# In a mixed attention and recurrence kernel, two of the four copies that carry a turned tile across the partitions go from ScalarE to VectorE

## The chip, the cores and the metric

The kernel runs on one core of one Trainium2 chip. The time is device microseconds of one execution, as median of several: 3127.36 us before the change (3 runs, 3123.82 to 3134.74). One further execution was recorded by the hardware profiler; all rows below are of that one. A core has five engines that this text speaks of: TensorE (PE, its weight loads PEld), VectorE (DVE), ScalarE (ACT), GpSimd (POOL) and SyncE (SP, which issues most DMAs). Each runs its own list of instructions in order and waits at semaphores for the others.

## The reference

The program is a whole block of a network on a sequence of 1024 tokens, followed by a second one. Only one stage matters here, the RWKV-7 recurrence, run forward and backward over the sequence with 8 heads of 64 channels:

```python
def wkv7_scan(r, w, k, v, a, b, reverse):
    def step(state, inp):
        r_t, w_t, k_t, v_t, a_t, b_t = inp
        sa = jnp.einsum('bhvk,bhk->bhv', state, a_t)
        state = (state * w_t[:, :, None, :] + sa[..., None] * b_t[:, :, None, :]
                 + v_t[..., None] * k_t[:, :, None, :])
        return state, jnp.einsum('bhvk,bhk->bhv', state, r_t)
    _, out = lax.scan(step, s0, xs, reverse=reverse)
```

Beside it stands the latent attention of the same layer (8 heads, 8 blocks of 128 queries, softmax over 1024 keys). The two need nothing from each other. What follows (output projection, feed-forward network, second block) is dense matmuls.

## The kernel before

**The recurrence by chunks.** The sequence is cut into 8 tiles of 128 tokens, each two chunks of 64. Both directions ("ways", d = 0 and 1) go over the 8 tiles, way 1 in the other order. Inside a tile the recurrence becomes matrix algebra, and it needs the inverse of a triangular 64 x 64 matrix for each of the 16 pairs of chunk and head. The inverse is built by doubling: first blocks of 8 (steps `row0` to `spread`, on VectorE), then level 3, 4 and 5 (blocks of 16, 32, 64). A level lev has two steps. `Y`: TensorE multiplies (16 calls, 32 recorded matmuls, line 1422), VectorE masks the product (line 1656). `X`: TensorE multiplies again (line 1438, for level 5 line 1445), VectorE adds the product to the inverse (line 1663, for level 5 line 1667).

**The turn.** The inverse is wanted in both orientations, X and its transpose XT. Three times in a tile the present one is turned: after `spread` (step `X`, from XT to X), and with the steps `Y4` and `Y5` (from X to XT). `across_pe` (line 1350) makes four 128 x 128 transposes on TensorE into one PSUM bank. The result lies with heads and chunks crossed, so that it takes four copies of 64 partitions x 256 elements to bring it home, each from one half of the partitions to one half: `across_act` (line 1355), all four on ScalarE. The next matmul of that way waits for the fourth (`a.by(s, ..., 3)`), and so does whoever takes the PSUM bank next: the two ways share a ring of four banks (`wtake`).

There are 16 tiles (8 for each way), 3 turns in each, and so 48 turns and 192 copies.

**What sets the order.** Each engine's list is written by a planner (`slots`) that lays the steps of the two ways beside each other, way 1 thirteen steps behind way 0, and puts the parts of the attention between them (on TensorE `S` line 1795, `V` line 1806, `T` line 1818; on VectorE the maximum `M` line 1824 and the reciprocal `R` line 1827; on ScalarE the exponential line 1840, the scaling line 1844 and two copies lines 1835 and 1850). One round of 27 steps carries both ways over one tile; tables (`STEADY`, `HEAD`, `ENDING`) fix the order within a step for the steady part, the start and the end. A step's name calls the same step function on every engine, and an engine that has nothing to do in it writes nothing.

**Other steps in the text.** `scores` (TensorE line 1395, VectorE masks line 1611 x4), `PV` (TensorE line 1406, VectorE line 1618), `Nc` (lines 1626 to 1629), `mul` (lines 1598 to 1606), `S0` and `S1` (the state: TensorE 1506 and 1512, VectorE 1685, 1688 and, for half of the partitions, 1693), `post1` to `post3` (lines 1697 to 1723). At the end the next stage is mixed in: line 297 splits a weight panel, line 2136 makes `oalo`, line 2169 are its matmuls.

Of the kernel before, what the change touches and what calls it, by code (L numbers as in the profile page):

```python
# [213 lines left out]
def build(nc, A, out):  # L214
# [19 lines left out]
    def banks(aps):  # L234
        everything.append(Ring(aps))
        return everything[-1]
# [18 lines left out]
    def K(name, n, o=0):  # L255
        return cc[:, CC[name] + o:CC[name] + o + n]
# [981 lines left out]
    wring = banks(bank[0:4])  # L1238
# [48 lines left out]
    def cols(n):  # L1287
        return slice(64 * n, 64 * (n + 1))
# [7 lines left out]
    def part(ap, lev, s):  # L1296
        b_ = 1 << lev
        if len(ap.shape) == 2:
            return ap.rearrange("p (g s b) -> p g s b", s=2, b=b_)[:, :, s, :]
        return ap.rearrange("p h (g s b) -> p h g s b", s=2, b=b_)[:, :, :, s, :]  # L1300

    def packed(ap, lev):
        return ap[:, 0:256].rearrange("p (h g b) -> p h g b", h=8, b=1 << lev)
# [38 lines left out]
    def wtake(e, d, s, name, *empties):  # L1342
        ap, waits = wring.take((d, s, name), *empties)
        for w in waits:
            e.wait_ge(*w)
        return ap

    def across_pe(e, ap, M):
        for p in range(4):
            m = e.transpose(ap[:, 128 * p:128 * (p + 1)], M[:, :, :].rearrange("q h t -> q (h t)")[:, 128 * p:128 * (p + 1)], ident)  # L1350
        return m

    def across_act(e, M, ap, sig, *key):
        for n, (cc_, h) in enumerate(((0, 0), (1, 1), (0, 1), (1, 0))):
            e.activation(M[cols(cc_), :, :].rearrange("q (p h) t -> q p h t", h=2)[:, :, h, :],
                         ap.rearrange("q (p c t) -> q p c t", p=4, c=2)[cols(h), :, cc_, :], AF.Copy).then_inc(*sig.up(*key, n))

    def w_pe(e, d, s, c):
        x, t, v, a, g = D[d], t_w[d], v_w[d], a_w[d], g_w[d]
# [15 lines left out]
        if c == "turn":  # L1375
            for name, sig, empty in (("At", v, a), ("Rt", v, a), ("Bt", v, a), ("Kt", v, a)):
                ap = wtake(e, d, s, name, (empty, s, name + "T"))
# [6 lines left out]
        if c == "scores":  # L1384
            e.wait_ge(*a.by(s, "BtT"))
            for half in range(2):
                bb = [wtake(e, d, s, ("SC", half, h), (v, s, "SC", half, h)) for h in range(2)]
                for w, y in ((x.BT, 128), (x.KT, 0)):
                    if half == 0 and y == 0:
                        e.wait_ge(*a.by(s, "KtT"))  # L1390
                    for q in range(2):
                        p = 2 * half + q
# [5 lines left out]
        if c == "PV":  # L1398
            e.wait_ge(*v.by(s, "SC", 0, 1))
            ap = wtake(e, d, s, "PV", (a, s, "PV"))  # L1400
# [6 lines left out]
                                 start=True, stop=True)  # L1407
            m.then_inc(*t.up(s, "PV"))
        if c == "X":
            ap = wtake(e, d, s, "X", (a, s, "X", 3))  # L1410
            e.wait_ge(*v.by(s, "XT0"))
            across_pe(e, ap, x.XT).then_inc(*t.up(s, "X"))
        if c in ("Y3", "Y4", "Y5"):
            lev = int(c[1])
            if lev == 3:
                e.wait_ge(*a.by(s, "X", 3))
            else:
                e.wait_ge(*v.by(s, "X", lev - 1))
            ap = wtake(e, d, s, ("Y", lev), (v, s, "Y", lev))
            for i, (h, p) in enumerate(HH):  # L1420
                for cc_ in range(2):
                    m = e.matmul(ap[cols(cc_), 32 * i:32 * (i + 1)], x.SC[cols(cc_), p, BA, h, :],  # L1422
                                 part(x.X[cols(cc_), i, :], lev, d), start=True, stop=True)
            m.then_inc(*t.up(s, "Y", lev))
            if lev > 3:
                ap = wtake(e, d, s, ("XT", lev - 1), (a, s, "XT", lev - 1, 3))
                across_pe(e, ap, x.X).then_inc(*t.up(s, "XT", lev - 1))
        if c in ("X3", "X4", "X5"):
            lev = int(c[1])
            Y = x.Ys[lev]  # L1430
            e.wait_ge(*v.by(s, "Y", lev))
            if lev > 3:
                e.wait_ge(*a.by(s, "XT", lev - 1, 3))
            if lev < 5:
                ap = wtake(e, d, s, ("X", lev), (v, s, "X", lev))
                for i in range(8):
                    for cc_ in range(2):
                        m = e.matmul(ap[cols(cc_), 32 * i:32 * (i + 1)], x.XT[cols(cc_), i, :],  # L1438
                                     part(Y[cols(cc_), i, :], lev, d), start=True, stop=True)
                m.then_inc(*t.up(s, "X", lev))  # L1440
            else:
                ap = wtake(e, d, s, ("XT", lev), (v, s, "XT", lev))
                for i in range(8):
                    for cc_ in range(2):
                        m = e.matmul(ap[cols(cc_), 32 * i:32 * (i + 1)], Y[cols(cc_), i, :],
                                     part(x.XT[cols(cc_), i, :], lev, 1 - d), start=True, stop=True)
                m.then_inc(*t.up(s, "XT", lev))
# [44 lines left out]
        if c in ("S0", "S1"):  # L1492
            n = int(c[1])
            cc_ = n if d == 0 else 1 - n
            if n == 0:
                e.wait_ge(*v.by(s, "RG", 1))
            ap = wtake(e, d, s, ("S", n), (v, s, "S+", n))
# [18 lines left out]
    def w_act(e, d, s, c):  # L1516
# [38 lines left out]
        if c == "X":  # L1555
            e.wait_ge(*t.by(s, "X"))
            across_act(e, x.X, wring.bank(d, s, "X"), a, s, "X")
        if c in ("Y4", "Y5"):
            lev = int(c[1]) - 1
            e.wait_ge(*t.by(s, "XT", lev))  # L1560
            across_act(e, x.XT, wring.bank(d, s, ("XT", lev)), a, s, "XT", lev)
# [21 lines left out]
    def w_dve(e, d, s, c):  # L1583
        x, t, v, a, g = D[d], t_w[d], v_w[d], a_w[d], g_w[d]
# [57 lines left out]
        if c == "spread":  # L1642
            e.wait_ge(*v.by(s, "row", 7))
            if s:
                e.wait_ge(*t.by(s - 1, "WU", 1))
            e.tensor_tensor(x.XT[:, :, :].rearrange("p h (b t) -> p h b t", b=8),
                            x.Xc[:, :, None, :].broadcast_to([128, 8, 8, 8]),
                            K("bm", 64).rearrange("p (b t) -> p b t", b=8)[:, None, :, :].broadcast_to([128, 8, 8, 8]),
                            OP.mult).then_inc(*v.up(s, "XT0"))
        if c in ("Y3", "Y4", "Y5"):  # L1650
            lev = int(c[1])
            Y = x.Ys[lev]
            m = K("lmask", 32 >> lev, 7 * d + LMASK[lev])[:, None, :, None].broadcast_to([128, 8, 32 >> lev, 1 << lev])
            e.wait_ge(*t.by(s, "Y", lev))
            e.wait_ge(*g.by(s, "Y0", lev))
            e.tensor_tensor(part(Y, lev, d), packed(wring.bank(d, s, ("Y", lev)), lev), m,
                            OP.mult).then_inc(*v.up(s, "Y", lev))
        if c in ("X3", "X4", "X5"):
            lev = int(c[1])
            if lev < 5:  # L1660
                Xs = part(x.X[:, :, :], lev, d)
                e.wait_ge(*t.by(s, "X", lev))
                e.tensor_tensor(Xs, packed(wring.bank(d, s, ("X", lev)), lev), Xs, OP.add).then_inc(*v.up(s, "X", lev))
            else:
                Xs = part(x.XT[:, :, :], lev, 1 - d)
                e.wait_ge(*t.by(s, "XT", lev))
                e.tensor_tensor(Xs, packed(wring.bank(d, s, ("XT", lev)), lev), Xs, OP.add).then_inc(*v.up(s, "XT", lev))
# [10 lines left out]
        if c in ("S0", "S1"):  # L1678
            n = int(c[1])
            cc_ = n if d == 0 else 1 - n  # L1680
            q = cols(cc_)
# [195 lines left out]
    def way_calls():  # L1877
        made = [(0, "split")]
        for s in range(9):
            for c in BEFORE + BETWEEN + AFTER:  # L1880
# [105 lines left out]
    def scan_pe(e):  # L1986
        e.wait_ge(*v_pre.all())
        e.wait_ge(*a_pre.all())
        e.wait_ge(*v_gt.all())
        scan(e, "pe", w_pe, att_pe, tail_pe)  # L1990

    def scan_dve(e):
        pre_over(e)
        scan(e, "dve", w_dve, att_dve, tail_dve)
# [1506 lines left out]
```

## Time and profile before

| | us |
|---|---|
| median of 3 runs | 3127.36 |
| lowest and highest run | 3123.82, 3134.74 |
| the profiled execution | 3123.17 |
| its span (first to last instruction) | 3121.4 |
| TensorE busy | 3047.4 (98%) |
| VectorE busy | 2038.7 (65%) |
| ScalarE busy | 1126.4 (36%) |
| GpSimd busy | 410.6 (13%) |
| mean granted TensorE clock | 0.994 |

The recurrence with the attention beside it takes from about 540 to 1225 us of the span; the turns lie between 568 and 1202 us. A row of a timeline gives the start in us from the start of the span, the length in us, the engine, the line, the operation with its tiles (out<-in), the shape, and how many equal instructions it merges; behind it, in brackets, the idle time of the engine ahead of it, and who ended it. "issue" means that the engine waited for nothing that the profile shows. The length of a matmul is modelled, so between matmuls the starts are compared.

### The profile page before, as it was taken

How to read it: one execution, taken by the hardware profiler on the slowest of the kernel's cores; microseconds unless marked ns; L12 is line 12 of the kernel's file. 1: busy time of each engine (PE TensorE's matmuls, PEld its weight loads, DVE VectorE, ACT ScalarE, POOL GpSimd, SP SyncE). 2: the span in 40 equal slices, each digit the busy share in tenths (PEclk: the TensorE clock that was granted, in tenths of full speed). 3: DMA queues.
4: the chain of work that ended last, by engine and by line, in shares of the span. 5: the costliest groups of instructions: out<-in, count | busy, mean ns of one | idle time of the engine just before them, and what ended most of it. 6: DMA issues, size and time to landing. Idle time of an engine off the chain costs nothing.

```text
span 3121.4 us, 52257 instructions
## 1 busy us (share of the span) xinstructions
PE 3047.4 (98%) x21972; PEld 2482.2 (80%) x21972; DVE 2038.7 (65%) x3118; ACT 1126.4 (36%) x1667; POOL 410.6 (13%) x467
## 2 busy tenths in 40 slices
PE   7999999899999999999999999999999999999999
PEld 7887887677777777888888888888776888788887
DVE  5666554477777675546556555698789999664454
ACT  5222334566666553223222222200144333433332
POOL 0232442011110001402221221100000000100000
PEclk9999999999999999999999999999999999999999
DMA  4333666223232223425545553566511223223222
GB/s 153 122 136 102 218 225 208 66 76 91 75 94 77 80 93 114 155 81 211 194 189 202 198 195 146 229 248 252 201 68 68 94 95 108 90 88 121 107 94 81
DMA packets 121754, 424.98 MB, mean 136 GB/s; under 512 B 15536, under 2 KB 41776, under 8 KB 94128
## 3 DMA queue, kind: packets, MB, share of 16 engines
q1 hardware_dynamic: 86880, 295.26, 26.9%
q0 software_dynamic: 34640, 126.37, 11.0%
q8 instruction: 175, 2.87, 0.4%
q14 instruction: 59, 0.48, 0.1%
HBM read 311.48 MB, written 110.10 MB: 135 GB/s over the span
## 4 chain that ended last, share of the span: by engine, by line
PE 82%; DVE 10%; ACT 3%; issue 2%; POOL 1%; DMA 1%; SPq 0%; DVEq 0%; ACTq 0%; POOLq 0%
PE ps L2645 29%; PE ps L321 15%; PE ps L505 8%; PE ps L2453 4%; PE ps L1795 3%; PE ps L2355 3%; PE ps L1818 2%; DVE Yh L2846 2%; PE ps L1422 2%; PE ps L1806 2%; PE ps L2169 1%; PE ps L1028 1%; PE ps L1438 1%; PE ps L1382 1%; DVE wlo L297 1%
## 5 line engine op out<-in xcount | busy, mean ns | idle before, releaser
L293 ACT ACTIVATE whi<-raw 128x2048 fp32r<-128x2048 f32 x131 | 250.4, 1911 | 385.9 <-PE ps L2645 189.8
L297 DVE TENSOR_TENSOR wlo<-raw,whi 128x2048 fp32r<-128x2048 f32 x131 | 300.7, 2295 | 87.3 <-ACT whi L293 86.9
L2846 DVE SCALAR_TENSOR_TENSOR Yh<-uT,vc,Yh 128x512 f32<-128x512 f32 x472 | 335.6, 747 | 4.0
L2645 PE MATMUL ps<-Hh,whi 128*128 128x512 f32 x1024 | 317.1, 391 | 0.6 <-DVE wlo L297 0.6
L2645 PEld LDWEIGHTS ps<-Hh,whi 128*128 128x128 f32 x1024 | 192.1, 188 | 42.7 <-issue 1.9
L321 PE MATMUL ps<-Hhi,whi 128*128 128x512 f32 x672 | 206.9, 389 | 0.0
L321 PE MATMUL ps<-Hlo,whi 128*128 128x512 f32 x672 | 206.9, 389 | 0.0
L321 PE MATMUL ps<-Hhi,wlo 128*128 128x512 f32 x672 | 206.8, 389 | 0.0
L2645 PE MATMUL ps<-aHh,whi 128*128 128x512 f32 x512 | 199.7, 390 | 0.1
L2645 PE MATMUL ps<-Hh,wlo 128*128 128x512 f32 x512 | 199.2, 389 | 0.0
L2645 PE MATMUL ps<-aHh,wlo 128*128 128x512 f32 x512 | 199.2, 389 | 0.0
L2645 PE MATMUL ps<-aLh,whi 128*128 128x512 f32 x512 | 199.2, 389 | 0.0
L2645 PE MATMUL ps<-Gh,whi 128*128 128x512 f32 x576 | 180.3, 394 | 2.9 <-DVE wlo L297 2.9
L3030 DVE TENSOR_TENSOR xT<-ps,xT 128x512 f32<-128x512 f32 x256 | 168.8, 685 | 19.1 <-PE ps L2645 19.1
L505 PE MATMUL ps<-Hhi,whi 128*128 128x512 f32 (+1 forms) x512 | 163.1, 400 | 0.0
L505 PE MATMUL ps<-Hlo,whi 128*128 128x512 f32 (+1 forms) x512 | 158.6, 391 | 0.0
L505 PE MATMUL ps<-Hhi,wlo 128*128 128x512 f32 (+1 forms) x512 | 157.9, 390 | 0.0
L321 PEld LDWEIGHTS ps<-Hlo,whi 128*128 128x128 f32 x672 | 126.1, 188 | 26.2
L321 PEld LDWEIGHTS ps<-Hhi,whi 128*128 128x128 f32 x672 | 126.1, 188 | 26.2
L321 PEld LDWEIGHTS ps<-Hhi,wlo 128*128 128x128 f32 x672 | 126.1, 188 | 26.2
L3014 DVE TENSOR_TENSOR aLh<-rth,aHh 128x512 fp32r<-128x512 f32 x64 | 41.3, 687 | 143.9 <-ACT aHh L3008 143.8
L1795 PE MATMUL ps<-Kp,Qb 96*128 96x512 f32 x256 | 128.8, 626 | 5.6 <-ACT Pb L1840 4.2
(417 smaller groups left out, 6394.4 us busy)
## 6 DMA issues: line engine op xcount, KB each, us to landing
raw<-in_panels SPq DMA_DIRECT2D x131, 1024.0 KB, 4.8
whi<-sph SPq DMA_DIRECT2D x28, 1024.0 KB, 4.8
wlo<-spl SPq DMA_DIRECT2D x28, 1024.0 KB, 6.9
rwf<-F POOLq DMA_DIRECT2D x16, 1280.0 KB, 6.5
sraw<-in_panels POOLq DMA_DIRECT2D x40, 512.0 KB, 4.4
sph<-shi POOLq DMA_DIRECT2D x40, 512.0 KB, 4.5
spl<-slo POOLq DMA_DIRECT2D x40, 512.0 KB, 5.2
L<-rwf SPq DMA_DIRECT2D x16, 1024.0 KB, 6.4
```

What stands on the lines that cost most here:

```text
L293: e.activation(whi[i % 2][:, :], raw_of(i)[:, :], AF.Copy).then_inc(*a_hi.up(i))
L297: e.tensor_tensor(wlo[i % 2][:, :], raw_of(i)[:, :], whi[i % 2][:, :].bitcast(F32), OP.subtract).then_inc(*v_lo.up(i))
L321: m = e.matmul(aps[h][0:n1 - n0, :], w[wi][:, kc, n0:n1], mov[mi][:, kc, hs(h)], start=x == 0 and q == 0, stop=x == len(kcs) - 1 and q == 2)
L505: m = e.matmul(aps[h][0:n1 - n0, :], W[wi][:, kc, n0:n1], H2[mi][:, kc, hs(h)], start=kc == 0 and q == 0, stop=kc == 7 and q == 2)
L1422: m = e.matmul(ap[cols(cc_), 32 * i:32 * (i + 1)], x.SC[cols(cc_), p, BA, h, :], part(x.X[cols(cc_), i, :], lev, d), start=True, stop=True)
L1795: m = e.matmul(bank[4 + half], Qb[g % 3][:, h, :], Kp[k % 2][:, h, hs(half)], start=True, stop=True)
L1806: m = e.matmul(bank[7][64 * n:64 * n + 64, 128 * (w % 4):128 * (w % 4) + 128], Vp[(w // 8) % 2][:, i, 64 * n:64 * n + 64], PT[:, i, n, :], ...
L2355: m = e.matmul(aps[h], W[wi][:, kc, n0:n0 + 128], H2[mi][:, kc, hs(h)], start=kc == 0 and q == 0, stop=kc == 7 and q == 2)
L2453: m = e.matmul(ap, W[wi][:, kc, 128 * n:128 * n + 128], (aH, aL)[mi][b % 2][:, kc, :], start=kc == 0 and q == 0, stop=kc == 1 and q == 2)
L2645: m = e.matmul(ap, W[wi][:, kc, n0:n0 + 128], mov[mi][:, kc, :], start=x == 0 and q == 0, stop=x == len(kcs) - 1 and q == 2)
L2846: e.scalar_tensor_tensor(out=to, in0=x, scalar=w, in1=to, op0=OP.mult, op1=OP.add).then_inc(*v_e.up(*key))
L3030: e.tensor_tensor(xT[:, n, hs(h)], ring.bank("x", h, b, n), xT[:, n, hs(h)], OP.add).then_inc(*v_e.up("x", h, b, n))
```

## The change

The four copies are parted by the half of the partitions that they read. ScalarE keeps the two that read partitions 0 to 63, VectorE gets the two that read 64 to 127 (one of them writes the upper half, one the lower). Who waited for ScalarE's fourth copy now waits for ScalarE's second and VectorE's second. On VectorE the copies stand in step `X` (which it had not taken part in), and in `Y4` and `Y5` right behind the mask. The planner is not changed, except that VectorE's table of the end names step `X` of way 1's last tile.

```diff
     def across_act(e, M, ap, sig, *key):
-        for n, (cc_, h) in enumerate(((0, 0), (1, 1), (0, 1), (1, 0))):
+        for n, (cc_, h) in enumerate(((0, 0), (1, 0))):
             e.activation(M[cols(cc_), :, :].rearrange("q (p h) t -> q p h t", h=2)[:, :, h, :],
                          ap.rearrange("q (p c t) -> q p c t", p=4, c=2)[cols(h), :, cc_, :], AF.Copy).then_inc(*sig.up(*key, n))
+
+    def across_dve(e, M, ap, sig, *key):
+        for n, (cc_, h) in enumerate(((1, 1), (0, 1))):
+            e.tensor_copy(M[cols(cc_), :, :].rearrange("q (p h) t -> q p h t", h=2)[:, :, h, :],
+                          ap.rearrange("q (p c t) -> q p c t", p=4, c=2)[cols(h), :, cc_, :]).then_inc(*sig.up(*key, n))
...
         if c == "X":
-            ap = wtake(e, d, s, "X", (a, s, "X", 3))
+            ap = wtake(e, d, s, "X", (a, s, "X", 1), (v, s, "X0", 1))
...
             if lev == 3:
-                e.wait_ge(*a.by(s, "X", 3))
+                e.wait_ge(*a.by(s, "X", 1))
+                e.wait_ge(*v.by(s, "X0", 1))
...
             if lev > 3:
-                ap = wtake(e, d, s, ("XT", lev - 1), (a, s, "XT", lev - 1, 3))
+                ap = wtake(e, d, s, ("XT", lev - 1), (a, s, "XT", lev - 1, 1), (v, s, "XTc", lev - 1, 1))
...
             if lev > 3:
-                e.wait_ge(*a.by(s, "XT", lev - 1, 3))
+                e.wait_ge(*a.by(s, "XT", lev - 1, 1))
+                e.wait_ge(*v.by(s, "XTc", lev - 1, 1))
...
+        if c == "X":
+            e.wait_ge(*t.by(s, "X"))
+            across_dve(e, x.X, wring.bank(d, s, "X"), v, s, "X0")
...
+            if lev > 3:
+                e.wait_ge(*t.by(s, "XT", lev - 1))
+                across_dve(e, x.XT, wring.bank(d, s, ("XT", lev - 1)), v, s, "XTc", lev - 1)
...
-                -20: ((1, 7, "spread"), (0, 7, "RG"), (1, 6, "post2")), -19: (), -18: ((0, 7, "S0"), (1, 7, "Y3")),
+                -20: ((1, 7, "spread"), (0, 7, "RG"), (1, 6, "post2")), -19: ((1, 7, "X"),), -18: ((0, 7, "S0"), (1, 7, "Y3")),
```

Where this puts the copies is seen best at two places of VectorE's list. The first is in the steady part, once in every round: the `scores` masks of way 1 (tile SC1), then the attention's maximum (st_m), `PV` of way 1 (E11), the level 3 mask of way 0 (Y30), `Nc` of way 1, and the level 3 addition of way 0 (X0). The number at the end of a name is the buffer's, a 0 or 1 ahead of it the way. Before:

```order
L1611 TENSOR_TENSOR SC1_156<-ps,cc_49 128x2x4x64 x4
L1824 TENSOR_REDUCE st_m_178<-ps 128x1
L1618 TENSOR_TENSOR E11_152<-SC1_156,cc_49 128x512
L1656 TENSOR_TENSOR Y30_124<-ps,cc_49 128x32x8
L1626 TENSOR_REDUCE Nc1_168<-E11_152 128x64
L1628 TENSOR_TENSOR Nc1_168<-Nc1_168,cc_49 128x64
L1629 COPY Xc1_169<-cc_49 128x64
L1663 TENSOR_TENSOR X0_122<-ps,X0_122 128x32x8
```

And in the changed kernel, whose line numbers are 7 to 13 higher:

```order
L1618 TENSOR_TENSOR SC1_156<-ps,cc_49 128x2x4x64 x4
L1360 COPY X0_122<-ps 64x4x64 x2
L1837 TENSOR_REDUCE st_m_178<-ps 128x1
L1625 TENSOR_TENSOR E11_152<-SC1_156,cc_49 128x512
L1666 TENSOR_TENSOR Y30_124<-ps,cc_49 128x32x8
L1633 TENSOR_REDUCE Nc1_168<-E11_152 128x64
L1635 TENSOR_TENSOR Nc1_168<-Nc1_168,cc_49 128x64
L1636 COPY Xc1_169<-cc_49 128x64
L1676 TENSOR_TENSOR X0_122<-ps,X0_122 128x32x8
```

The two copies of way 0's X stand behind the four masks and ahead of the maximum and of way 0's own mask. The second place is the end of the recurrence, on VectorE too: `post2` (sc1), the split of the next stage's weight panel (wlo0), the state of way 0 (St01), its output (Os0) and way 1's level 3 mask (Y31). Before:

```order
L1706 TENSOR_SCALAR sc1_167<-sc1_167 128x8
L297 TENSOR_TENSOR wlo0_56<-raw0_51,whi0_54 128x2048
L1685 TENSOR_TENSOR St01_139<-ps,H0_136 128x256
L1688 TENSOR_TENSOR St01_139<-St01_139,sc0_140 128x256
L1693 TENSOR_TENSOR Os0_137<-ps,Os0_137 64x4x64 x2
```

And in the changed kernel:

```order
L1719 TENSOR_SCALAR sc1_167<-sc1_167 128x8
L1360 COPY X1_149<-ps 64x4x64 x2
L297 TENSOR_TENSOR wlo0_56<-raw0_51,whi0_54 128x2048
L1698 TENSOR_TENSOR St01_139<-ps,H0_136 128x256
L1701 TENSOR_TENSOR St01_139<-St01_139,sc0_140 128x256
```

The copies, which wait for TensorE's transposes, now stand ahead of the panel's split, which waited for ScalarE alone.

## Rows read from the trace of the kernel before

**Rows 1.** Windows: length, busy (x) of PE, PEld, DVE, ACT, POOL; clock, DMA share, GB/s.
```profile
800.00:880.00 80.00, 78.87 (x1420) 63.10 (x1418) 56.44 (x124) 50.94 (x97) 8.00 (x11) 1.00 0.29 88
...
1060.00:1080.00 20.00, 16.40 (x302) 13.35 (x304) 11.72 (x27) 9.57 (x21) 0.21 (x1) 0.83 0.38 118
```
**Rows 2.** Line 1355, copies into XT: duration ns min/median/max, first and last start, forms.
```profile
L1355 ACT ACTIVATE XT<-ps x128: 375/378/381, 582.2 to 1200.5; 64x256 f32<-64x256 f32 x128
```
**Rows 3.** VectorE's copy of line 1671, same columns.
```profile
L1671 DVE COPY WU<-ps x16: 691/692/692, 603.7 to 1206.6; 128x512 f32<-128x512 f32 x16
```
**Rows 4.** Timeline of VectorE, 819 to 833 us, and one row at 982 us.
```profile
819.56 2.48 DVE L1611 TENSOR_TENSOR SC<-ps,cc 128x512 f32<-128x512 f32 x4 [0.58 <-PE ps L1395]
...
823.09 0.68 DVE L1618 TENSOR_TENSOR E<-SC,cc 128x512 f32<-128x512 f32 x1
823.81 0.42 DVE L1656 TENSOR_TENSOR Y<-ps,cc 128x256 f32<-128x256 f32 x1
...
826.41 0.42 DVE L1688 TENSOR_TENSOR St<-St,sc 128x256 f32<-128x256 f32 x1
826.87 0.77 DVE L1693 TENSOR_TENSOR Os<-ps,Os 64x256 f32<-64x256 f32 x2
827.67 0.42 DVE L1656 TENSOR_TENSOR Y<-ps,cc 128x256 f32<-128x256 f32 x1
...
831.70 0.42 DVE L1688 TENSOR_TENSOR St<-St,sc 128x256 f32<-128x256 f32 x1
832.04 0.74 DVE L1693 TENSOR_TENSOR Os<-ps,Os 64x256 f32<-64x256 f32 x2
832.71 0.41 DVE L1656 TENSOR_TENSOR E<-ps,cc 128x256 f32<-128x256 f32 x1
...
981.86 0.42 DVE L1656 TENSOR_TENSOR Y<-ps,cc 128x256 f32<-128x256 f32 x1 [0.36 <-PE ps L1422]
```
**Rows 5.** Timeline of TensorE: one round earlier, and beside the first rows of group 4.
```profile
743.89 1.12 PE L1422 MATMUL ps<-X,SC 64*64 64x32 f32 x32
...
822.64 1.12 PE L1422 MATMUL ps<-X,SC 64*64 64x32 f32 x32
...
824.29 1.12 PE L1438 MATMUL ps<-Y,XT 64*64 64x32 f32 x32
```
**Rows 6.** Timeline, VectorE and TensorE, around way 1's step X.
```profile
855.08 0.69 DVE L1606 TENSOR_TENSOR Kt<-L,E 128x512 f32<-128x512 f32 x1
...
856.49 1.12 PE L1422 MATMUL ps<-X,SC 64*64 64x32 f32 x32
```
**Rows 7.** Timeline, ScalarE and TensorE, around way 1's last turn of a tile.
```profile
873.77 1.58 ACT L1355 ACTIVATE XT<-ps 64x256 f32<-64x256 f32 x4 [1.80 <-PE ps L1350]
...
874.74 0.66 PE L1818 MATMUL ps<-cc,Pb 128*128 128x128 f32 x4
875.50 1.12 PE L1445 MATMUL ps<-XT,E 64*64 64x32 f32 x32
```
**Rows 8.** Timeline of TensorE in the first tile of way 0.
```profile
572.20 1.12 PE L1422 MATMUL ps<-X,SC 64*64 64x32 f32 x32 [0.75 <-ACT X L1355]
...
593.91 0.67 PE L1395 MATMUL ps<-AR,BT 64*64 64x128 f32 x16 [0.73 <-ACT XT L1355]
```
**Rows 9.** Timeline of TensorE, two gaps that nothing in the profile ends.
```profile
985.81 0.54 PE L1422 MATMUL ps<-X,SC 64*64 64x32 f32 x13 [0.89 <-issue]
...
1068.82 1.91 PE L1422 MATMUL ps<-X,SC 64*64 64x32 f32 x30 [3.26 <-issue]
```
**Rows 10.** Timeline at the end of the recurrence, TensorE and VectorE.
```profile
1159.94 1.12 PE L1445 MATMUL ps<-XT,E 64*64 64x32 f32 x32 [0.69 <-ACT XT L1355]
...
1169.89 2.32 DVE L297 TENSOR_TENSOR wlo<-raw,whi 128x2048 fp32r<-128x2048 f32 x1
1170.23 0.65 PE L1350 MATMUL ps<-cc,XT 128*128 128x128 f32 x4
...
1187.38 0.73 PE L2169 MATMUL ps<-oalo,whi 128*128 128x512 f32 x2 [0.40 <-DVE oalo L2136]
```

## The prediction

> **What bounds the kernel.** First the windows: in a steady stretch of 80 us TensorE is busy for 78.87, VectorE for 56.44, ScalarE for 50.94 [rows 1]. TensorE has some 1.1 us in 80 to give back, so halving a copy's latency can bring little. Harm has more room: whatever makes TensorE wait lengthens the span one for one. Next the copies themselves: ScalarE takes 378 ns for one [rows 2] and 1.58 us for four [rows 7]. Then the timelines of TensorE and VectorE around each of the six turns of one round (both ways, one tile each; 743.89 to 822.64, 78.75 us [rows 5]), to see what ends last ahead of the next matmul. The stretch that matters is VectorE's from 819.56 to 828.09: from the masks of `scores` on it is never idle (the bracket at 819.56 is the last until 829.62) [rows 4], and TensorE's level 3 matmuls start right on its heels: the mask of line 1656 ends at 823.81 + 0.42 = 824.23 and line 1438 starts at 824.29 [rows 4, 5]. Here VectorE is the bound, though it is busy for only 71% of the 80 us.
>
> **What the change removes.** 96 copies leave ScalarE, 96 x 0.378 = 36 us of its time, and a turn's latency there falls from 1.58 to about 0.78. ScalarE ends few waits of TensorE, so this pays only at the places named below.
>
> **What a copy costs VectorE.** The trace has no such copy there. Bounds: the addition of line 1693 has the same size, reads PSUM, and takes 0.77 or 0.74 for two, 0.41 each with the overlap [rows 4]; the copy of twice the elements takes 0.69 [rows 3]. The new copy reads one input, so I take 0.42, near line 1693; the range is 0.35 to 0.69.
>
> How close do they follow each other? Two rows of the same pair of instructions answer: in way 1's `S0` line 1688 starts at 826.41 and line 1693 at 826.87, 0.46 later; in `S1` it is 831.70 and 832.04, 0.34 later. The instruction behind starts 0.80 after line 1693 in the first case (827.67) and 0.67 in the second (832.71) [rows 4]. By the code (`q = cols(cc_)`) the first works on partitions 64 to 127, the second on 0 to 63, and all around them start at partition 0. So a change of the half costs 0.12 to 0.13 going in and as much coming out. Both new copies read the upper half, one writes the upper and one the lower, and their neighbours start at partition 0: each copy starts only when what precedes it has ended, and so does the next instruction that reads PSUM. I take 0.46 from copy to copy and to the next PSUM reader, and 0.12 ahead of the first where it has not waited anyway: 2 x 0.46 + 0.12 = 1.04 us of VectorE's list for a pair ahead of a PSUM reader, instead of 2 x 0.34 = 0.68.
>
> The Trainium skill (VectorE: DVE Perf Modes, Two Vector instructions with no wait between them) says the same as a rule: an instruction is held until all earlier ones have finished if its input or output begins in another quadrant of 32 partitions than the last one's did. The trace agrees, by the 0.46 against 0.34. With the rule the sum is the one below, +4.6 us; without it, +1.2.
>
> **Steady rounds, turn by turn.**
>
> Way 0's step X (tiles 1 to 4). The masks of line 1611 end at 819.56 + 2.48 = 822.04. In the new list the pair stands behind them: 822.08 to 822.95. TensorE's line 1422 started at 822.64 [rows 5] and now starts at 823.01, +0.37. But the maximum, line 1618 and the level 3 mask, back to back in front of line 1438, move by 1.04; the mask had waited 0.12 (823.81 against 823.09 + 0.60), so it comes 0.92 later, and line 1438 with it. The rest of VectorE's run follows at the same distance, so nothing is caught up: 4 x 0.92 = +3.7. The attention's maximum is 1.04 late as well, and ScalarE's exponential with it; TensorE's next `S`, which waits for the exponential, stands behind levels 3 and 4 and doesn't notice.
>
> The same step in tiles 5 and 6. There the mask waits 0.36 for TensorE (981.86) [rows 4], the delay would be 0.6 (1.04 less the 0.36 and its start-up), and soon after TensorE stands still for 0.89 and 3.26 us with nothing to release it [rows 9]. I read these as waits for its own instructions: another 0.6 us of lateness disappears in them. I take 0, with both ends at the third rival. In tile 7 no maximum follows, and I take 0.
>
> Way 1's step X. The pair stands behind line 1606, which ends at 855.77: 855.81 to 856.68. Line 1422 started at 856.49 [rows 6] and now at 856.74: +0.25, seven times: +1.75. The pair delays besides only `R`, which isn't urgent: ScalarE has four copies of `turn` to do before it scales.
>
> Way 1's step Y5. TensorE's line 1445 started at 875.50, when ScalarE's four copies were done at 873.77 + 1.58 = 875.35; the transposes of line 1818 end by their modelled length at 874.74 + 0.66 = 875.40, and what is behind them can start 0.1 before that modelled end or right at it [rows 7]. VectorE's pair ends at about 874.65, in time. Between 0.10 and 0.20 are won, I take 0.15: 7 x -0.15 = -1.05.
>
> The other three turns of a round have a long group of attention matmuls (`S` or `V`) behind them, and the pair ends before it does: 0.
>
> **Start.** In tile 0 of way 0 VectorE is idle, and TensorE waits 0.75 and 0.73 for line 1355 [rows 8]. Both waits nearly go: -0.6 and -0.7, -1.3.
>
> **End.** At 1159.94 TensorE waited 0.69 for the copies [rows 10], and gets 0.38 of it back, since the pair, in VectorE's list ahead of way 1's `S1`, makes the level 5 addition about 0.3 later (my estimate from 2 x 0.46). Then line 297, which started at 1169.89, must wait behind the copies for TensorE's transposes at 1170.23 + 0.65, 0.38 earlier by then: 1170.50, copies to 1171.4, so line 297 starts 1.57 late. The state and output behind it absorb most, but 0.3 reaches level 3, and the next pair (level 3 into XT) with its 1.1 us stands ahead of `post3` and line 2136, for which TensorE waits until 1187.38 [rows 10]: together +1.4 to +1.5 there, against the level before this stretch. I take +1.45; with the second pair hidden it would be +0.3.
>
> **The sum.** 3.7 + 0 + 1.75 - 1.05 - 1.3 + 1.45 = +4.55 us. TensorE also gets 48 more wait instructions; the profile shows no price for one ahead of a matmul that is queued in time, and I take 0, at most 0.02 each, 1 us. The profiled execution took 3123.17 (the span and 1.8 around it), which makes 3127.7. The median shown is 4.2 above it, since the runs lie between 3123.82 and 3134.74; from it the sum gives 3131.9. I say 3130, between the two.
>
> **Rivals.**
>
> *VectorE takes them in its stride.* If copies follow at 0.34 as `S1`'s neighbours do, the steady places cost 4 x (0.68 - 0.12) = 2.2 and 7 x 0.1 = 0.7, the end 0.6, the gains stay at -2.35: +1.15, or, with tiles 1 to 4 covered by something unseen, -1: 3122 to 3126. For it: 23 us of idle VectorE in 80. Against it: the two distances in rows 4. 17%.
>
> *Slower: VectorE's list is the bound, not only at one turn.* A pair (1.04, or 1.6 with the 0.69 copy) reaches TensorE at way 0's step X in all six tiles and at way 1's step X in full: 6 x 0.92 + 7 x 1.04 + 1.45 - 1.3 - 1.05 = +11.9 us, 3135 to 3141. It decides where `turn`'s and `scores`' ScalarE copies are not ready before the delayed matmul, or where a copy takes over 0.5 us. For it: the run without idle time. Against: around 856 only line 1422 stands behind the pair. 18%.
>
> *The two unexplained gaps move.* The one at 1068.82 is dear: the granted clock of its 20 us is 0.83 [rows 1], so for (1 - 0.83) x 20 / 0.5 = 6.8 us of them TensorE was at 1.2 instead of 2.4 GHz, after it had idled for 3.26. That is at most 3.26 + 3.4 = 6.7 us, of which I take 6. The added waits move TensorE's instruction stream by some places against its loads. If this gap goes, the sum is -1.5, 3121 to 3126; if another such one comes, +10.5, 3134 to 3138. For it: both gaps fall into the same matmul group of neighbouring rounds [rows 9], so place matters. Against: the stream moves by under 50 instructions. 13%.
>
> **Chances.** 52% for the forecast with its own range of 3125 to 3136, 17, 18 and 13 for the rivals. The range of 8 in 10 is 3120 to 3141. A difference under 0.3% (9.4 us) can't be told from none in this kernel. Slower by more than that is most of the second rival, part of the third and a tail of the forecast, 0.20; faster needs the first rival and a vanished gap together, 0.07; within it 0.73.
>
> **What will show it.** A pair of copies that takes 0.87 to 0.9 us from start to end and is followed at 0.46 by the maximum; VectorE's level 3 mask of way 0 starting about 5.2 us after the first of the four score masks did, instead of 4.25; an idle time of TensorE ahead of line 1438's successor of about 0.5 us, ended by VectorE, in tiles 1 to 4, and none in other steady turns; a round of 79.8 instead of 78.75 us; line 1445 0.15 us closer to the transposes before it; ScalarE's busy time 36 us less, VectorE's 40 more. The forecast is wrong if a copy takes over 0.6 us, if the round stays at 78.75, or if the 3.26 us gap isn't there.

## The result and the profile after

The changed kernel took 3137.86 us (median of 18 runs, 3125.72 to 3152.9), the kernel before 3129.26 (18 runs, 3116.76 to 3138.18): ratio 1.0034, 95% interval [1.0021, 1.0047]. By the ratio that is 10.6 us slower (interval 6.6 to 14.7; the two medians lie 8.6 apart), where the forecast's sum was +4.55. The time lies in the range of 3120 to 3141, but outside the forecast's own 3125 to 3136. What came is the second rival, VectorE's list being the bound at more than one turn (+11.9, 3135 to 3141), to which 18% was given.

The profiled execution of the changed kernel took 3133.26 us, its span 3131.5. ScalarE is busy for 1091.0 us and VectorE for 2078.8. In the window of [rows 1] TensorE lost 1.47 us of busy time and VectorE gained 4.99:

```profile
800.00:880.00 80.00, 77.40 (x1392) 61.55 (x1389) 61.43 (x136) 45.04 (x84) 8.00 (x11) 1.00 0.27 83
```

The new copies, in the columns of [rows 2]. A VectorE copy takes 427 ns, 0.42 was taken:

```profile
L1360 DVE COPY XT<-ps x64: 425/427/428, 581.2 to 1210.2; 64x256 f32<-64x256 f32 x64
L1360 DVE COPY X<-ps x32: 425/427/428, 568.9 to 1178.7; 64x256 f32<-64x256 f32 x32
```

Way 0's step X, the stretch of [rows 4] (lines of VectorE's steps have moved, 1656 to 1666, 1611 to 1618, 1824 to 1837; TensorE's 1422 to 1428 and 1438 to 1445). Timeline of VectorE, changed kernel (start and length in us, engine, line, operation, and in brackets the idle time before it and what ended it):

```profile
819.24 2.48 DVE L1618 TENSOR_TENSOR SC<-ps,cc 128x512 f32<-128x512 f32 x4 [0.58 <-PE ps L1400]
821.75 0.88 DVE L1360 COPY X<-ps 64x256 f32<-64x256 f32 x2
822.67 1.23 DVE L1837 TENSOR_REDUCE st_m<-ps 128x1 f32<-128x1024 f32 x1
823.81 0.68 DVE L1625 TENSOR_TENSOR E<-SC,cc 128x512 f32<-128x512 f32 x1
824.41 0.42 DVE L1666 TENSOR_TENSOR Y<-ps,cc 128x256 f32<-128x256 f32 x1
```

and TensorE beside it:

```profile
822.74 1.12 PE L1428 MATMUL ps<-X,SC 64*64 64x32 f32 x32 [0.28 <-issue]
823.79 0.66 PE L1831 MATMUL ps<-cc,Pb 128*128 128x128 f32 x4
824.88 1.12 PE L1445 MATMUL ps<-Y,XT 64*64 64x32 f32 x32 [0.43 <-DVE Y L1666]
```

The pair takes 0.88, the maximum starts 0.92 after the pair did (two pitches of 0.46), and the level 3 mask starts 824.41 - 819.24 = 5.17 us after the first score mask (5.2 forecast, 4.25 before). TensorE has two idle times there that it did not have, 0.28 and 0.43. The profile names nobody for the first, but VectorE's pair ends at 821.75 + 0.88 = 822.63 and line 1428, which waits for it, starts at 822.74. Counted from the first score mask, the matmuls behind the level 3 mask start after 824.88 - 819.24 = 5.64 us, before the change after 824.29 - 819.56 = 4.73: +0.91.

Way 1's step X, the stretch of [rows 6], TensorE and VectorE:

```profile
854.82 0.66 PE L1387 MATMUL ps<-cc,AP 128*128 128x128 f32 x4 [0.20 <-ACT E L1539]
855.31 0.60 PE L1387 MATMUL ps<-cc,Rt 128*128 128x128 f32 x4
855.87 0.63 PE L1387 MATMUL ps<-cc,SC 128*128 128x128 f32 x4
857.34 0.63 PE L1387 MATMUL ps<-cc,Kt 128*128 128x128 f32 x4 [0.84 <-DVE X L1360]
```
```profile
855.64 0.68 DVE L1613 TENSOR_TENSOR Kt<-L,E 128x512 f32<-128x512 f32 x1
856.35 0.88 DVE L1360 COPY X<-ps 64x256 f32<-64x256 f32 x2
```

This wait was not forecast. TensorE's transposes of Kt start when VectorE's second copy has ended (856.35 + 0.88 = 857.23). The reason is in the code: both ways take their PSUM banks from one ring of four, in the order in which TensorE's program asks. Way 1's X takes a bank, way 0's At, Rt and Bt (AP, Rt and SC in the rows) the other three, and Kt comes round to the one that X is still being copied from. The waits of TensorE over the whole span (us in total, times, longest) show it seven times, and a second new wait six times:

```profile
PE ps L1387 <- DVE X L1360: 5.9, 7, 0.8
...
PE ps L1445 <- DVE Y L1666: 2.6, 6, 0.4
```

The steady round is measured here from one tile of way 1 to its next, between the starts of the "spread transposes" (line 1350 reading XT, which is step X behind `spread`). Timeline of TensorE, before, then changed:

```profile
695.95 0.63 PE L1350 MATMUL ps<-cc,XT 128*128 128x128 f32 x4 [0.28 <-DVE XT L1646]
774.68 0.63 PE L1350 MATMUL ps<-cc,XT 128*128 128x128 f32 x4 [0.20 <-DVE XT L1646]
853.43 0.63 PE L1350 MATMUL ps<-cc,XT 128*128 128x128 f32 x4 [0.20 <-DVE XT L1646]
```
```profile
693.37 0.63 PE L1350 MATMUL ps<-cc,XT 128*128 128x128 f32 x4 [0.27 <-DVE XT L1653]
773.72 0.63 PE L1350 MATMUL ps<-cc,XT 128*128 128x128 f32 x4 [0.21 <-DVE XT L1653]
853.99 0.63 PE L1350 MATMUL ps<-cc,XT 128*128 128x128 f32 x4 [0.21 <-DVE XT L1653]
```

78.73 and 78.75 before, 80.35 and 80.27 changed: +1.6 a round, where +1.05 was forecast.

The gaps of [rows 9] (idle times of TensorE that the profile puts to "issue") are not the same ones. The 3.26 us one is gone (there is one of 0.49 at 1078.18, ahead of another line), and near the 0.89 one stands:

```profile
989.30 1.71 PE L1428 MATMUL ps<-X,SC 64*64 64x32 f32 x28 [1.08 <-issue]
```

with half the clock behind it, which before's 990 to 1000 did not have (windows, columns as in [rows 1]):

```profile
990.00:1000.00 10.00, 10.00 (x115) 7.40 (x115) 4.49 (x9) 1.96 (x4) 0.00 (x0) 0.50 0.27 66
```

### The profile page after: what moved, and what is told of

Read it like the earlier page. It is cut to its first block, busy times and chain, and to the rows that moved or that the text cites. A ratio compares the mean times of both kernels' runs of the same rounds, so it can differ in the third digit from the quotient of the medians.

```text
span 3131.5 us, 52305 instructions
## 1 busy us (share of the span) xinstructions
PE 3051.8 (97%) x21972; PEld 2487.2 (79%) x21972; DVE 2078.8 (66%) x3214; ACT 1091.0 (35%) x1571; POOL 410.6 (13%) x467
## 4 chain that ended last, share of the span: by engine, by line
PE 79%; DVE 13%; issue 3%; ACT 3%; POOL 1%; DMA 1%; SPq 0%; DVEq 0%; ACTq 0%; POOLq 0%
PE ps L2658 29%; PE ps L321 15%; PE ps L505 7%; PE ps L2466 4%; PE ps L1808 3%; PE ps L2368 3%; DVE Yh L2859 2%; PE ps L1819 1%; PE ps L1428 1%; PE ps L2182 1%; PE ps L1831 1%; PE ps L1028 1%; PE ps L1445 1%; DVE wlo L297 1%; DVE st_m L1837 1%
```

## The experiments

What has to be told apart is what a profile alone leaves mixed: the price of each pair, and gaps and clock. "Round" is the steady round as above. In the expectations A is the theory that step X's two places hold the loss and XT's pairs are free, B that every pair on VectorE costs alike. Each of the kernels is compared in times with the kernel before on its own chip.

**Step X on ScalarE alone, XT split.** In all variants of this kind a function says for which ways and steps the copies are parted, and waits follow it:

```diff
+    def parted(d, s, step):
+        return False if step == "X" else True
-            across_act(e, x.X, wring.bank(d, s, "X"), a, s, "X")
+            across_act(e, x.X, wring.bank(d, s, "X"), a, s, "X", both=parted(d, s, "X"))
-        if c == "X":
+        if c == "X" and parted(d, s, "X"):
             e.wait_ge(*t.by(s, "X"))
```

> The XT copies stay split, step X is back on ScalarE alone (four copies there) in both ways. The measure is the steady round, the distance between the spread transposes of successive tiles (L1350): 78.75 us in the kernel before, 80.3 us changed. Theory A (PSUM bank and list): of the +1.6 us a round about 0.8 us is the wait of PE's Kt transposes for the two VectorE copies of way 1's step X (0.84 us at 857.34), about 0.75 us is VectorE's list behind way 0's pair, and the XT pairs cost nothing: round 78.6 to 78.9 us here. Rival B (VectorE's load as such: six pairs a round, each at a like price of 0.27 us): round 79.8 us. Rival C (the round is not what matters, only the two issue gaps around 985 and 1075): total as in the changed kernel. In total under A: 5 to 8 us under the changed kernel if the gap at 989 goes, else 4 to 5 us over that; and as tile 0's gain at the start (4 us under C's and A's count alike) hangs on tile 0's step X, the total would be within 3 us of the kernel before.

Ratio 0.9994 [0.9978, 1.0011], 12 runs. Rounds of 78.61 and 78.58 in the profile, and 79.25 in the one that has an issue gap (0.28 at 697.08), which explains less than half of the difference. A holds, B (79.8) falls: 32 pairs on VectorE cost nothing in the round. The two short rounds are 0.15 under before's 78.74, the size of the forecast's term for way 1's Y5, but the time as a whole is not told apart from before's.

```profile
612.22 0.63 PE L1350 MATMUL ps<-cc,XT 128*128 128x128 f32 x4 [0.88 <-DVE XT L1662]
690.83 0.63 PE L1350 MATMUL ps<-cc,XT 128*128 128x128 f32 x4 [0.28 <-DVE XT L1662]
```

**Step X split in way 0 only** (`return d == 0 if step == "X" else True`).

> Step X is split in way 0 only, way 1's four copies are on ScalarE as before, XT split in both. Theory A: no PE wait for VectorE's X copies at the Kt transposes (changed kernel: 5.9 us in 7 waits), way 0's price of about 0.75 us stays: round 79.4 to 79.6 us against 80.3. Rival B (each pair alike at 0.27): round 80.0 us, and the wait at the Kt transposes may go without the round getting shorter, because VectorE's list would be the next to be late. Start gain of tile 0 (4 us by the first spread transpose, 613.11 against 617.15) kept if it is way 0's, gone if it is way 1's.

Ratio 1.0024 [1.0009, 1.004]. Rounds 79.54, 80.00, 79.50: the two short ones are 0.92 above the last kernel's short ones (78.60), which is the price forecast for this turn. For the 80.00 its profile shows no further wait; rounds of one profile differ by up to some 0.5 us in this way, so a price read from them is good to a few tenths. The wait at the Kt transposes is gone (its row has no bracket), so A's reading of that place holds:

```profile
859.54 0.63 PE L1390 MATMUL ps<-cc,Kt 128*128 128x128 f32 x4
```

**Step X split in way 1 only** (`d == 1`).

> Step X is split in way 1 only, XT split in both. Theory A: the wait at the Kt transposes stays (about 0.8 us, 7 times), the waits behind way 0's pair (PE L1445 for VectorE's SC, 0.4 us in 6 places) go: round 79.5 to 79.7 us. Rival B: 80.0 us.

Ratio 1.0021 [1.0005, 1.0037]. Rounds 79.50, 79.30, 79.59: 0.85 above 78.6, as A has it. The waits behind way 0's pair are gone, that at Kt stays (from 690 to 1010 us):

```profile
PE ps L1390 <- DVE X L1363: 3.4, 4, 0.8
```

**The halves exchanged.**

```diff
-        for n, (cc_, h) in enumerate(((1, 1), (0, 1))):
+        for n, (cc_, h) in enumerate(((0, 0), (1, 0))):
             e.tensor_copy(...)
```

ScalarE takes the other two, (1, 1) and (0, 1).

> The same split as in the changed kernel, but the engines change halves: VectorE copies what lies in the lower PSUM partitions, ScalarE the upper. If the hold between instructions that change the half of the partitions (pitch 0.46 against 0.34 us) is what delays the list behind way 0's pair, that saves one such change there, 0.12 us: masks at 5.05 us behind the first score mask (5.17 changed), round 80.1 to 80.2 us. If the hold is of no weight here: 80.3 us, the same total.

Ratio 1.0034 [1.0017, 1.0051]. Rounds from 80.15 to 80.88: in the time the small term isn't told apart. In the places it is there. Timeline of VectorE:

```profile
824.47 2.48 DVE L1627 TENSOR_TENSOR SC<-ps,cc 128x512 f32<-128x512 f32 x4 [0.58 <-PE ps L1403]
826.86 0.86 DVE L1363 COPY X<-ps 64x256 f32<-64x256 f32 x2
827.75 1.23 DVE L1846 TENSOR_REDUCE st_m<-ps 128x1 f32<-128x1024 f32 x1
829.49 0.42 DVE L1675 TENSOR_TENSOR Y<-ps,cc 128x256 f32<-128x256 f32 x1
```

The mask starts 829.49 - 824.47 = 5.02 us after the first score mask (5.05 expected, 5.17 in the changed kernel), and the wait at the Kt transposes is 0.70 instead of 0.84; one hold less would give both. Part of it goes into another wait of the round (line 1840 for ScalarE's PT, 0.66; 0.52 in the changed kernel).

**One instruction earlier in way 1.**

```diff
+            if d == 0 and s:
+                w_dve(e, 1, s - 1, "early")      # way 1's two copies
             e.tensor_tensor(x.Kt[:, :], k_, x.E2[:, :], OP.mult).then_inc(*v.up(s, "Kt"))
...
-        if c == "X":
+        if c == ("early" if d and s < 7 else "X"):
```

> The changed kernel; in way 1 VectorE makes step X's two copies one instruction earlier, ahead of way 0's Kt product instead of behind it. If the PSUM bank alone were what TensorE's Kt transposes wait for, the copies' earlier end (0.6 us) would shorten the wait from 0.84 to about 0.2 us and the round from 80.3 to 79.7 us. If it is VectorE's list (the transposes want the bank and the product, and VectorE makes both), the wait is then for the Kt product and stays 0.7 to 0.8 us, the round 80.2 us.

Ratio 1.0025 [1.0004, 1.0046], rounds 80.31 and 80.32. The bank is free earlier, and the same transposes now wait as long for the product, which VectorE makes behind the copies. Timeline of TensorE and of VectorE:

```profile
866.46 0.63 PE L1387 MATMUL ps<-cc,Kt 128*128 128x128 f32 x4 [0.89 <-DVE Kt L1615]
```
```profile
864.84 0.89 DVE L1360 COPY X<-ps 64x256 f32<-64x256 f32 x2
865.64 0.68 DVE L1615 TENSOR_TENSOR Kt<-L,E 128x512 f32<-128x512 f32 x1
```

So the bank is only where it shows. VectorE has to make four products and two copies before these transposes, and which of the last two comes first doesn't matter; on ScalarE the copies lay beside the products.

**Step X split in both ways, XT on ScalarE alone** (`return step == "X"`).

> Step X is split in both ways, XT is on ScalarE alone. If prices add (way 0's step X 0.83 us a round by e_x0 less e_xt, way 1's 0.53 by e_x1 less e_xt, XT 0.18 by e_xt less the kernel before): round 78.74 + 0.83 + 0.53 = 80.1 us, ratio 1.003. Rival (VectorE's load at large): a third of the pairs of a round, 78.74 + 1.57/3 = 79.3 us, ratio 1.001.

Ratio 1.0025 [1.0008, 1.0041]. Rounds of 80.49 and 80.46 without a gap over 0.3 us, others longer by gaps of up to 2.3; 80.1 was expected from the sum, 79.3 by load. Load falls; the sum is near, a little low. With the prices as read from the short rounds, 0.92 and 0.85, it is 78.74 + 0.92 + 0.85 = 80.5.

**The issue gaps.** Waits were put at the very start of TensorE's program, where it stands idle for 13.7 us, to move its instruction stream. That idle time was too short for them. In the ten profiles without them TensorE's first matmul starts between 12.56 and 13.86 us, with 322 of them at 20.87, with 250 at 17.13 and 16.90; so 72 waits more take some 3.8 us, 0.05 each. The delay is still there at 520 us: the attention's first `S` starts at 528.5, 524.0 and 523.4 us, against 519.2 to 521.3 in the others. The ratios of the three padded kernels therefore hold 7 and 4 us (0.23% and 0.13%) that have nothing to do with gaps.

```diff
     def mla_pe(e):
+        for _ in range(322):
+            e.wait_ge(*d_vec.by())
```

> The kernel before, with 322 further waits (161 instructions) at the start of TensorE's program, on a load that has landed long before its first matmul at 13.7 us; nothing else is changed. Theory F: the issue gaps (0.89 us at 985.81, 3.26 us at 1068.82) come where TensorE's instruction stream reaches a certain count (I count 256 instructions between such places) while a large load is under way, so a program moved by 161 instructions has none there, and keeps the clock behind them: 7 us less than before (ratio 0.9977), the profile without a gap over 0.5 us from 960 to 1100. Rival: the gaps belong to the place in the work or are chance: the same gaps or others like them, ratio 0.999 to 1.001.

Ratio 1.0012 [0.9993, 1.0031]; less the 7 us of late start it would be some 0.999 ±0.002, and there neither theory F's 0.9977 nor the rival's 0.999 to 1.001 is excluded. From 960 to 1100 us there is indeed no gap, but there are eight from 635 to 952 instead, 0.34 to 0.97 long, such as

```profile
678.40 0.88 PE L1424 MATMUL ps<-X,SC 64*64 64x32 f32 x23 [0.97 <-issue]
```

Moving the stream moved the gaps. What they take in all in this one profile, 5.0 us between 540 and 1225, is not less than before's 4.1. Whether the expected 7 us were there, this kernel can't show.

The same in the changed kernel (250 waits):

> The changed kernel with 250 further waits (125 instructions) at the start of TensorE's program. Theory F: no gap at 989 (1.08 us) and 1078 (0.49 us), full clock from 990 to 1010, 5 to 7 us less than the changed kernel (ratio to before 1.0012 to 1.0018), while the round stays 80.3 us: the round, not the gaps, holds what the change costs. Rival (the change's loss lies in the gaps, which only its extra instructions moved): ratio to the kernel before 1.000. Rival (gaps are chance): 1.0034 as the changed kernel.

Ratio 1.003 [1.0009, 1.0051], less the 4 us of late start some 1.0018. That is the upper end of theory F's range, but with ±0.002 the rival's 1.0034 isn't excluded. Rounds 80.20 and 80.28: no gap is left from 960 to 1100 and the round is as long as ever, so what the round costs isn't in those gaps. But now the clock fell at another place, without any long gap ahead of it (windows):

```profile
820.00:830.00 10.00, 9.22 (x200) 7.55 (x200) 8.85 (x19) 5.62 (x10) 2.07 (x4) 0.93 0.64 225
830.00:840.00 10.00, 10.00 (x116) 7.39 (x112) 4.82 (x10) 3.10 (x6) 0.00 (x0) 0.50 0.15 38
```

And with step X on ScalarE:

> Step X on ScalarE alone, XT copies split, and 250 further waits at the start of TensorE's program. Theory F with theory A: round 78.7 to 78.9 us, no gap over 0.5 us between 960 and 1100: ratio to the kernel before 0.997 to 0.9985, the fastest of all. Rival (gaps are chance): 0.9994 as without the waits.

Ratio 1.0005 [0.9984, 1.0025], rounds 79.16, 79.04 and 78.97, and a gap of 2.24 at 948.77. Less the late start this is some 0.999, which again lies between theory F's 0.997 to 0.9985 and the rival's 0.9994. That no gap over 0.5 us stands from 960 to 1100 came true; a gain isn't shown.

**Two repeats.** First all copies on ScalarE again (`return False`), then the changed kernel.

> All copies on ScalarE, as in the kernel before: the same instructions in the same order. If the two issue gaps of the kernel before (0.89 us at 985.81, 3.26 us at 1068.82) come from the program's layout, they come again at these places within 0.5 us of their length; if they are chance in place or length, this profile has others, and the steady round is 78.7 us either way.

Ratio 0.999 [0.9978, 1.0003]. A round of 78.82, and gaps in the same instruction stream of which the first is not before's:

```profile
705.62 3.78 PE L1817 MATMUL ps<-Kp,Qb 96*128 96x512 f32 x4 [3.02 <-issue]
...
996.40 0.54 PE L1434 MATMUL ps<-X,SC 64*64 64x32 f32 x13 [1.99 <-issue]
...
1077.22 1.11 PE L1434 MATMUL ps<-X,SC 64*64 64x32 f32 x30 [0.80 <-issue]
```

The last two stand ahead of the same pieces, x13 and x30, as in [rows 9], but are 1.99 and 0.80 long where they were 0.89 and 3.26. Three more, of 0.87, 1.04 and 0.36 us, stand at 626.34, 916.48 and 1034.05, where before had none. So a gap can come again at its place with another length, and others come and go. The length varies from run to run; the program may set where a gap can be, but not that there is one.

> The changed kernel once more, for its profile. Round 80.3 us again, wait at the Kt transposes 0.84 us again. The first spread transpose at 613.1 us if tile 0's gain is the change's, up to 618 us if it hung on the clock there; a gap near 989 us and half the clock behind it again if they are the program's, elsewhere if not.

3145.79 us in one run. The 1.08 us gap near 989 is not there. Rounds 80.21 and 80.27, Kt waits 0.8 each; way 1's first spread transpose at 615.73. From 630 to 1080 us no issue gap is over 0.28, and yet the clock is at half twice, behind the same turn of two tiles (windows):

```profile
670.00:680.00 10.00, 10.00 (x113) 7.39 (x112) 4.82 (x10) 2.70 (x6) 0.00 (x0) 0.50 0.15 38
...
920.00:930.00 10.00, 10.00 (x112) 7.39 (x112) 4.85 (x11) 1.96 (x4) 0.00 (x0) 0.50 0.15 38
```

**The clock apart from the rest.** Every run has its time and its mean granted clock. Their product is roughly what the run would take at full clock, and the rest what the clock took; the clock is recorded to 0.001, or 3 us a run, so only means say something. Means over the runs, with the standard error of the mean:

| kernel | runs | time x clock | lost to the clock |
|---|---|---|---|
| before (three chips) | 93 | 3105.0 to 3105.6, each ±0.6 or less | 21.7 to 23.1 ±1.1 |
| all on ScalarE again | 10 | 3105.1 ±0.7 | 20.6 ±1.4 |
| XT split alone | 12 | 3104.9 ±0.5 | 19.8 ±1.6 |
| way 0's X and XT | 12 | 3107.6 ±0.7 | 26.7 ±1.9 |
| way 1's X and XT | 12 | 3110.3 ±0.5 | 21.9 ±1.5 |
| X alone, both ways | 12 | 3114.6 ±0.6 | 21.4 ±2.3 |
| changed | 19 | 3112.6 ±0.6 | 26.3 ±1.6 |
| halves exchanged | 12 | 3112.1 ±0.7 | 24.8 ±1.5 |
| one instruction earlier | 12 | 3111.7 ±0.2 | 23.3 ±1.4 |
| before, 322 waits | 12 | 3112.1 ±0.5 | 18.0 ±1.5 |
| changed, 250 waits | 12 | 3112.9 ±0.7 | 22.8 ±2.4 |
| XT split alone, 250 waits | 12 | 3106.5 ±0.7 | 20.9 ±2.0 |

Against XT alone, way 1's step X costs 5.4 us of full-clock time and 2.1 ±2.2 of clock, way 0's 2.7 and 6.9 ±2.5. Together 8.1 of full-clock time, and the changed kernel has 7.7: the prices add. Against before the changed kernel has 7.3 us more of full-clock time, which stands well outside the errors (the two variants of it that ran on one chip with the kernel before, halves exchanged and one instruction earlier, have 6.5 and 6.7), and 4.0 ±1.7 more of clock. The clock's share is the weaker one. The five other kernels with way 0's step X split lose between 21.4 and 26.7 us to it. All 79 runs with that step split, the changed kernel's among them, lose 24.4 ±0.8, all 151 without 21.5 ±0.5: 2.9 ±0.9, and not 6.9, is what way 0's step X takes through the clock over all kernels. The 7 us of full-clock time of "before, 322 waits" are its late start.

## Why the prediction came out as it did

- **Copy, pitch, list of way 0: right.** 0.427 for 0.42, 0.46 for 0.46, the mask at 5.17 for 5.2, the matmuls behind it 0.91 later for 0.92, and 0.92 a round by the experiment. That an instruction is held when its input or output begins in another quadrant of 32 partitions than the last one's, as the Trainium skill (VectorE: DVE Perf Modes, Two Vector instructions with no wait between them) says, agrees with the 0.46 here and with the exchange of halves, which has one such change less and put the mask at 5.02. That this hold matters for the time the exchange couldn't show.
- **Way 0, tiles 5 and 6 taken as 0: wrong.** The new wait of 0.43 is there six times, at 986.05 and 1076.08 too. That the gaps would hide the lateness was argued from [rows 9]; 2 x 0.92 = 1.8 us were missed by it, if a round there pays what a steady one does.
- **Way 1's step X, 7 x 0.25: the step that failed.** The forecast put only line 1422 behind the pair, and wrote against its rival that "around 856 only line 1422 stands behind the pair". Between Kt's product and line 1422 stand the Kt transposes, and they need the bank that the pair reads. Measured: 5.9 us in seven waits, 0.85 a round by experiment, so 7 x 0.85 = 5.95 for 1.75, which is 4.2 us missed. Two rows of the kernel before that the forecast did not use, TensorE's and ScalarE's, had it:

```profile
855.92 0.63 PE L1382 MATMUL ps<-cc,Kt 128*128 128x128 f32 x4
```
```profile
854.13 1.59 ACT L1355 ACTIVATE X<-ps 64x256 f32<-64x256 f32 x4
```

  ScalarE's four copies had freed the bank at 855.72, 0.2 ahead of the transposes. The new pair can't start before VectorE's products are done at 855.77 [rows 6].
- **Way 1's Y5, -0.15 each: right in size.** The matmuls of line 1452 now start 0.58 us after the transposes ahead of them (876.67, 876.09), 0.76 before: -0.18. The round with XT alone split is 0.15 shorter than before's.
- **Start, -1.3: about right.** Both waits of [rows 8] are gone. The 4 us by which way 1's first spread transpose came earlier in the profile (613.11 for 617.15) are not the change's: between 580 and 590 us the clock was 0.86 instead of 0.51. With the clock at a like level there (0.52 and 0.54) the repeats of both kernels have 615.73 and 616.79, -1.1; counted from way 0's first spread transposes, at 568.37 and 567.54, it is -1.9.
- **End, +1.45: not contradicted.** From line 1350 of the last tile (1099.47, 1106.61) to the span's end it is 2021.9 before and 2024.9 changed, +3.0, of which 1.5 are the clock's at 1180 to 1190 (0.85). The wait of 0.69 at 1159.94 is gone, a new one of 0.79 stands at 1181.81, ended by `St`, and the four at line 2182 have 0.63 as the longest. The same stretch takes 2021.5 and 2023.4 in the other two profiles with all copies on ScalarE, and from 2022.9 to 2027.3 in the others with pairs on VectorE, so no run tells 1.45 from 0.3 or from 3.
- **The gaps as a rival: half right.** Their places move with the stream, but the two runs of one stream gave other lengths and partly other places, so a case built on one profile's gap vanishing or not was no property of the change.
- **The signs.** The forecast named three that would show it wrong, and one of them came: the 3.26 us gap isn't there. After the repeats this says nothing on the copies. The signs that did speak were two others: a wait of 0.84 in another steady turn, where none was forecast, and a round of 80.3 for 79.8. To a kernel slower by more than 0.3%, which is what came (0.34%), it had given 0.20.

With the two steps mended the sum is 4.55 + 1.8 + 4.2 = +10.6, and the ratio gives +10.6. That the two agree so closely is luck: the sum has waits alone, of which the runs show 7.3 us of full-clock time, and the clock's share of 4.0 ±1.7 was in no term. So the mended sum is some 3 us too high for the waits, and where that lies stays open. Of the 48 more wait instructions, taken as 0 and at most 0.02 each, no run shows the price in the steady part; at the start of the program one took 0.05.

No version here beats the kernel before: XT alone is level with it.

## What to carry to other kernels

Before a step is moved to a busier engine, list for each place everything that must be done before the next thing TensorE does, the holders of its PSUM banks too, and not only the reader of what the step writes. A buffer taken in turn makes whoever comes round next a consumer of the slowest reader. And measure a change of a third of a per cent by the steady round and by one-place variants: a single profile's span carries several microseconds of gaps and clock that are no part of the change. Where a test adds instructions, look first when the work behind them starts: here they cost as much as what they were to find.

## What the hardware showed that was not expected

- Issue gaps of TensorE from 0.3 to 3.3 us, whose places change with the instruction stream (322 waits put ahead of it moved them), some of which come again in a second run of one stream, with other lengths (3.26 and 0.80, 0.89 and 1.99), beside new ones.
- A wait at a semaphore that has long been reached took TensorE some 0.05 us (72 more of them at the start of its program, 3.8 us later).
- The granted clock falls to 0.50, the 1.2 GHz level, both behind long gaps (700 to 720 behind 3.02, some 10 us in all) and without one (820 to 850, some 17 us). Between 600 and 1050 us there are five such falls without a gap above 1.1 us ahead of them, each some 17 us long. All are in kernels with way 0's step X split, in four of the seven profiles of such kernels, and all behind the turn in which TensorE now idles for 0.28 and 0.43 (in the changed kernel's first profile 0.43 and 1.08) while the DMA share is 0.63 to 0.65. Gaps of 2.24 at 948.77 and of 1.99 at 996.40 brought no fall. That these idle times are what lowers the clock fits the 2.9 ±0.9 us of all runs, but was not tested by itself.
- One kernel's 35 runs on one chip spread from 3111 to 3148 us, and most of that is the clock's (0.997 and 0.988 in these two).
